# Two transformer blocks with a 32-expert layer: experts scattered in pairs, down weights laid out by partition, the first units split row by row, feed-forward features multiplied by the norms as they leave their banks

## The reference, cut to what matters

```python
# first block, x: 256 tokens by 1024
h = rms_norm(x, norm_mix);  z = h @ w_in                  # gated unit and differential attention
x = x + concat(a_out, o) @ w_out
x = x + memory_attention(rms_norm(x, norm_xq), rms_norm(mem, norm_mem), ...)
h = rms_norm(x, norm_ffn)                                 # 32 experts, 4 groups of 8
# the best group, its best two experts; wts = gate_g * pe_top / sum(pe_top)
y_e = (silu(h @ w_gate[e]) * (h @ w_up[e])) @ w_down[e]   # 1024 -> 512 -> 1024, chosen tokens only
x = rms_norm(x + sum_k wts[k] * y_ek, norm_final)
# second block
u = block_attention(rms_norm(x, norm_mix_pre_2));  h = x + rms_norm(u, norm_mix_post_2)
u = square(relu(rms_norm(h, norm_ffn_pre_2) @ w_up_2)) @ w_down_2    # 1024 -> 4096 -> 1024
out = h + rms_norm(u, norm_ffn_post_2)
```

## Time and profile before

| | |
|---|---|
| median of 3 runs | 1034.48 us (1034.04 to 1034.89) |
| the profiled execution | 1031.15 us, span 1029.7 us |
| PE, PEld, DVE, ACT, POOL busy | 94%, 63%, 40%, 33%, 2% |
| HBM read | 287.90 MB, 281 GB/s over the span |

### The profile page before, as it was taken

One profiled execution on the slowest core, in us unless ns is written; L12 is line 12 of the kernel. 1 busy time (PEld: TensorE's weight loads), 2 busy tenths in 40 slices (PEclk: granted clock), 3 DMA queues, 4 the chain that ended last, 5 costly groups with the idle time before them and its releaser, 6 DMA issues.

```text
span 1029.7 us, 13765 instructions
## 1 busy us (share of the span) xinstructions
PE 967.3 (94%) x5479; PEld 646.3 (63%) x5479; DVE 416.4 (40%) x721; ACT 339.4 (33%) x556; POOL 24.1 (2%) x40
## 2 busy tenths in 40 slices
PE   5999989998899999999999999997999969999997
PEld 4979878985433343333433334332898859998885
DVE  4756565445221212212222122223564655665434
ACT  7635436533111111111111111114464545454332
POOL 1300000000000000000000000000000000000000
PEclk9989999998999999999999999998999989999999
DMA  9943443486799999999999999999545525555501
GB/s 323 353 137 123 164 134 143 157 301 274 307 416 425 423 419 421 425 424 418 421 425 419 420 424 425 420 420 362 188 164 164 164 85 175 171 202 169 201 1 41
DMA packets 84047, 289.59 MB, mean 281 GB/s; under 512 B 4897, under 2 KB 44449, under 8 KB 75810
## 3 DMA queue, kind: packets, MB, share of 16 engines
q1 hardware_dynamic: 83426, 288.79, 73.3%
q10 hardware_dynamic: 576, 0.17, 0.1%
HBM read 287.90 MB, written 1.05 MB: 281 GB/s over the span
## 4 chain that ended last, share of the span: by engine, by line
PE 87%; DVE 6%; ACT 3%; issue 2%; POOL 1%; DMA 0%; DVEq 0%; SPq 0%; ACTq 0%
PE bank L1482 22%; PE bank L425 14%; PE bank L426 14%; PE bank L427 13%; PE bank L1503 11%; PE bank L1456 5%; PE bank L1514 2%; PE bank L1493 1%; DVE routeT L1578 1%; DVE w_low L506 1%; PE bank L708 1%; PE bank L746 1%; PE bank L467 1%; DVE arena L1577 1%; ACT w_high L477 1%
## 5 line engine op out<-in xcount | busy, mean ns | idle before, releaser
L506 DVE TENSOR_TENSOR w_low<-ring,w_high 128x2048 fp32r<-128x2048 f32 x78 | 178.9, 2294 | 135.2 <-ACT w_high L477 135.2
L1482 PE MATMUL bank<-ring,arena 128*64 128x512 f32 x1024 | 227.0, 595 | 0.0
L477 ACT ACTIVATE w_high<-ring 128x2048 fp32r<-128x2048 f32 x78 | 149.4, 1916 | 127.3 <-PE bank L427 127.3
L1482 PEld LDWEIGHTS bank<-ring,arena 128*64 128x64 f32 x1024 | 74.0, 138 | 145.1 <-issue 144.9
L1503 PE MATMUL bank<-ring,arena 128*64 128x512 f32 x512 | 116.9, 599 | 0.5 <-issue 0.5
L425 PE MATMUL bank<-xT_high,w_high 128*128 128x256 f32 x384 | 110.1, 287 | 2.4 <-DVE xT_low L515 2.4
L427 PE MATMUL bank<-xT_high,w_low 128*128 128x256 f32 x384 | 109.3, 285 | 0.0
L426 PE MATMUL bank<-xT_low,w_high 128*128 128x256 f32 x384 | 109.2, 284 | 0.0
L1588 DVE SCALAR_TENSOR_TENSOR y_low<-bank,arena,y_high 128x512 fp32r<-128x512 f32 x32 | 24.0, 751 | 135.8 <-ACT y_high L1545 135.8
L1584 DVE TENSOR_TENSOR arena<-bank,arena 128x256 f32<-128x256 f32 x32 | 13.6, 424 | 160.5 <-ACT arena L1534 160.5
L1534 ACT ACTIVATE arena<-bank 128x256 f32<-128x256 f32 x32 | 12.3, 384 | 196.4 <-PE bank L1482 196.4
(11 more groups left out here) (270 smaller groups left out, 1453.9 us busy)
## 6 DMA issues: line engine op xcount, KB each, us to landing
ring<-in_w_gate SPq DMA_DIRECT2D x32, 2048.0 KB, 18.6
ring<-in_w_up SPq DMA_DIRECT2D x32, 2048.0 KB, 23.1
ring<-in_w_down SPq DMA_DIRECT2D x32, 2048.0 KB, 21.7
ring<-in_w_up SPq DMA_DIRECT2D x16, 1024.0 KB, 5.7
ring<-in_w_down SPq DMA_DIRECT2D x16, 1024.0 KB, 4.9
ring<-in_attn_w_qkv SPq DMA_DIRECT2D x12, 1024.0 KB, 11.9
ring<-in_w_in SPq DMA_DIRECT2D x10, 1024.0 KB, 11.1
ring<-in_w_kv_mem SPq DMA_DIRECT2D x8, 1024.0 KB, 5.3
```

The costliest lines, as they stand in the source:

```text
L477: SC.activation(parts[buffer[0][u]][0][:, :], lanes[n % len(lanes)], ACT.Copy).then_inc(*high.inc(u))
L506: DVE.tensor_tensor(p[1][:, :], lanes[n % len(lanes)], p[0][:, :].bitcast(F32), ALU.subtract).then_inc(*split.inc(u))
L1482: last = PE.matmul(GU[t * SLOTS:(t + 1) * SLOTS, 0:NGU], xs[:, k, :], wgu[:, :, k, t * (DE // JT):(t + 1) * (DE // JT)], start=k == 0, sto ...
```

## The change

**Start.** The first two units are split in four rows of 512 columns each, with semaphores of their own, and PE starts with the first row; the second group of chunks of the tokens is written after that. `u0` is multiplied before the memory tokens are transposed.

**Experts.** The scatter works on pairs of experts. The route of a pair is built as three blocks of 64 slots (first, second, first expert), so that one transpose gives both experts above each other in 128 partitions. `down` of the second expert of a pair writes its halves exchanged, and `y` is kept by column half, with the two experts in 64 partitions each. A pair is scattered in the step after it, with matmuls of 128 partitions. The route transposes stand before `gate_up`, and the gather's pieces in four steps of six (three steps have a gather and no scatter). `y_high` and `y_low` become two instructions of 64 partitions each.

**Down weights.** They are laid out by partition on the host, as gate and up are: one run of 16 KB for each partition.

**Second feed-forward.** The sums are transposed without their norms. The norms are spread over partitions (`norm_wide`), transposed on PE after `f1` (bank `r2`) and kept as a row `row2`. DVE writes relu times norm out of the bank in one instruction (`norm_kept`), and ACT squares this twice, once into a float32 tile and once as the high part. The sum of squares of a bank's first half is taken when that bank is closed, and the mean is formed before the second gain.

```diff
+fT00@4 fT01@5 fT10@6 fT11@7 f0 f1 r2 f2 f3 f4 f5 f6 f7 f8 f9 f10 f11 f12 f13 f14@0 f15@7
...
-    w_down = a["w_down"][0].rearrange("e (c p) n -> e p c n", p=P)
+    w_down = a["w_down"]
...
-    for name in ("w_gate", "w_up"):
+    for name in ("w_gate", "w_up", "w_down"):
         laid[name] = np.stack([by_partition(w) for w in np.asarray(inputs[name])[0]])
...
+                    if row_ready and h == halves[0]:
+                        PE.wait_ge(*row_ready[c])
...
+        def rows_high(u):
+            n = order1.index(u)
+            SC.wait_ge(lane1_sem[n], 16)
+            for c in range(4):
+                o = slice(512 * c, 512 * (c + 1))
+                done = row_high.inc(f"{u}{c}") if c < 3 else high1.inc(u)
+                SC.activation(parts1[buffer1[0][u]][0][:, o], lanes1[n][:, o], ACT.Copy).then_inc(*done)
...
-        turned_highs(bank1, "hT", 0, hT[0], G_MIX)
-        high("v.0")
-        turned_highs(bank1, "hT", 1, hT[0], G_MIX)
-        high("v.1")
+        turned_highs(bank1, "hT", 0, hT[0], G_MIX, groups=(0,))
+        rows_high("v.0")
+        turned_highs(bank1, "hT", 1, hT[0], G_MIX, groups=(0,))
+        turned_highs(bank1, "hT", 0, hT[0], G_MIX, groups=(1,))
+        turned_highs(bank1, "hT", 1, hT[0], G_MIX, groups=(1,))
+        rows_high("v.1")
+        high("u0")
...
-            o = (t * NY) % 512
-            for y in YS:
...
-                                 tile_position=(t * SLOTS, 0), skip_group_check=True)
+            for y in Y[t]:
+                last = PE.matmul(ACC[2 * h + t][:, :], ROUTET[:, b, t, h, :], y[:, :], start=False, stop=True,
+                                 skip_group_check=True)
...
+        turn_route(q, n, b, odd, pair + 1, n)
...
-        if more and s:
-            gather_even(q, trio + 1, 2 * s - 2, 1 - buffer)
-        if more:
-            turn_route(q, n + 1, (j + 1) % 3, n)
-        scatter(q, n - 1, (j + 2) % 3, 0, False)
-        turn_hidden(q, n, n + 2 if more else n + 1)
-        scatter(q, n - 1, (j + 2) % 3, 1, True)
-        if more and s:
-            gather_odd(q, trio + 1, 2 * s - 1, 1 - buffer)
...
+        if p is not None:
+            gather_even(q, trio + 1, p, 1 - buffer)
+        if not odd:
+            scatter(q, n, n, (b + 2) % 3, 0, False)
+        turn_hidden(q, n, n + 1)
+        if not odd:
+            scatter(q, n, n, (b + 2) % 3, 1, True)
+        if p is not None:
+            gather_odd(q, trio + 1, p + 1, 1 - buffer)
...
+        for i in range(JT):
+            p, t = slice(i * SLOTS, (i + 1) * SLOTS), i ^ odd
+            last = SC.activation(Y[t][0][p, :], DN[p, 0:NY], ACT.Copy, scale=SLOT_WEIGHT[p, b, t:t + 1])
...
+        for i in range(JT):
+            p, t = slice(i * SLOTS, (i + 1) * SLOTS), i ^ odd
+            last = DVE.scalar_tensor_tensor(out=Y[t][1][p, :], in0=DN[p, 0:NY], scalar=SLOT_WEIGHT[p, b, t:t + 1],
+                                            in1=Y[t][0][p, :].bitcast(F32), op0=ALU.mult, op1=ALU.subtract)
+        last.then_inc(*q.inc("y"))
...
-            square_sum(X[:, h, :], XN[:, h, :], f"pre{h}", stat("pre", h))
-            scale_half("pre", h, XN, X)
...
-            SC.activation(scratch(2 * (i % 2)), banks[bank2.bank[f"f{i}"]][:, :], ACT.Relu).then_inc(*relu_done.inc(i))
...
-            SC.activation(hidden_parts[0][:, 512 * i:512 * (i + 1)], scratch(2 * (i % 2) + 1), ACT.Copy).then_inc(*sq_high.inc(i))
+            SC.activation(square, kept, ACT.Square)
+            SC.activation(hidden_parts[0][:, 512 * i:512 * (i + 1)], kept, ACT.Square).then_inc(*sq_high.inc(i))
...
-            DVE.tensor_tensor(scratch(2 * (i % 2) + 1), banks[bank2.bank[f"f{i}"]][:, :], scratch(2 * (i % 2)),
-                              ALU.mult).then_inc(*bank2.inc(f"f{i}"))
...
+            DVE.scalar_tensor_tensor(
+                out=scratch(2 * (i % 2)).rearrange("p (n t) -> p n t", t=S),
+                in0=banks[bank2.bank[f"f{i}"]][:, :].rearrange("p (n t) -> p n t", t=S), scalar=0.0,
+                in1=row2.rearrange("p (n t) -> p n t", n=1).to_broadcast([P, 2, S]), op0=ALU.max,
+                op1=ALU.mult).then_inc(*bank2.inc(f"f{i}"))
...
+                if j == 1:
+                    DVE.tensor_scalar(s[:, 0:1], s[:, 0:1], s[:, 1:2], RMS_EPS, ALU.add,
+                                      ALU.add).then_inc(*meansq.inc(f"{tag}{h}"))
```

380 lines of the change are left out of this document (223 added, 157 removed).

## The result

The changed kernel takes 1016.94 us (median of 4 runs, 1015.87 to 1017.38), the kernel before 1034.26 in the same comparison (1033.57 to 1034.89). The ratio is 0.9844, 95% interval 0.9827 to 0.9861: faster by 1.6%. Forecast were 1025.0 and a range of 1019.5 to 1031.0. The sign was right, the size too small, and the range did not hold the time.

A forecast was written before the change was run, and what follows sets the result against it. PE bounds the kernel, but the experts' loads leave only 2.0 us of slack. From 1031.15, −2.7 − 7.8 + 2.0 + 0.7 − 1.7 = −9.5 gives 1021.6, and the step to the median 1025.0; range 1019.5 to 1031.0.

The forecast's parts named there:

- the landing of the last `w_up`: End of the experts' stage: lands at 687.7 and starts the last `gate_up`, 10.5 us earlier, 7.8 the experts' own.
- the price of the feed-forward's loop: Second feed-forward: period 6.1 for 5.76, 0.37 more in 13 turns, 0.7 in the last two; whole part +0.7 us.
- Bound and mechanism: Experts: of PE's saving only 2.0 us of slack count unless transfers get faster; the last `w_up` sets the end.
- The third rival: Pairing and layout both buy nothing, freed time goes to new waits: −1.7 us, 1032.8; chance 0.08.
- the first (the layout buys nothing): Rival in the experts' loads: down piece no faster, last `w_up` 5.0 later, total −4.5 us, 1030.0; chance 0.13.
- The second, nothing of the start given back and a shorter loop: Rival at start and feed-forward: start keeps all, loop keeps 5.9 (−1.3 − 3), about 1020.5 us; chance 0.13.
- The down piece: Experts' loads: a down piece takes 4.92 us in place of 5.10, 5.0 us over 28 experts.
- the experts' two rates: Experts: PE saves 0.5 us for each, then waits for DMA about 0.85 us each in the last eight or so.
- The start: First matmul of `v.0` 3.4 us earlier, at 11.9; 0.7 given back behind it, so −2.7 us net.
- The tail: Behind the last `down`: doubled `y_high` and `y_low` cost 0.60 and 0.75, last scatter 0.6; 2.0 us later.
- From the profile to the median: Last step of the sum: 3.3 us added because before's median lay above its profiled execution, 1021.6 to 1025.0.
- The slower rival: Feed-forward loop: PE stands about 0.6 us each turn, clock drops, 15 turns cost 20 us, 1045; chance 0.06.

The follow-up runs named there:

- the four corners of layout and pairs: Kernels with neither, the new layout alone, pairs alone (changed, old layout), or both; first to last `gate_up` took 446.58, 446.14, 442.99 and 436.39 us.
- the run with half of the scatter: Changed kernel with the scatter of the low parts of `y` left out; 1020.12 us, ratio to the kernel before 0.9873.
- before's second profile: The kernel before, run again with a profile and no edit; 1032.3 us (one run).
- the changed kernel's second profile: The changed kernel, run again with no edit; 1015.58 us, ratio to the kernel before 0.9828.

## Why the prediction was right in sign and wrong in size

Four steps of the sum failed, against 8.1 us of miss: the landing of the last `w_up` (687.7, it was 685.8), PE's own saving in the experts (0.5 us for one, it was 0.33), the price of the feed-forward's loop (7.75 us given back, it was 4.5), and the 3.3 us added from the profile to the median (it was −0.4). The experts' own part, to which the first two belong, came out 2.4 better than forecast, the loop 3.2 and the step to the median 3.8; the other terms took 1.3 back.

**Bound and mechanism: right, by 0.3 us.** The last `gate_up` starts at the landing of the last `w_up`, as forecast, though PE stands only 0.33 us for it. That PE's saving alone counts little more than the slack, and that the layout is what turns it into time, is shown by the four corners of layout and pairs and by the run with half of the scatter. The third rival (both buy nothing) and the first (the layout buys nothing) are out. The second, nothing of the start given back and a shorter loop, came in its second half.

**The down piece: right, a little small.** Forecast 4.92 in place of 5.10, measured 4.89 in place of 5.11 (medians of the landings from 290 us on). The step from there to the stage failed: "The last `w_up` then lands at 696.2 − 2.7 − 0.8 − 5.0 = 687.7". It landed at 685.83. The 696.2 was one execution's, and held 1.5 us of a disturbance at 348 and 1.0 more at 287; the same kernel's second profile lands at 694.63. The down pieces gave 6.2 in place of 5.0. Against these, the queue began to fill only 1.5 us earlier (261.13 in place of 262.62), where 3.5 were forecast. 687.7 − 2.5 − 1.2 + 2.0 is 686.0, close to what was measured. A landing late in a filled queue carries every gap ahead of it, and gaps should be taken out before it is used as a base.

**PE alone: the experts' two rates, wrong.** 0.5 us for an expert was forecast, 0.33 measured (83.75 for six). The route's transposes cost 0.47 in place of 0.4, the steps that only gather 3.1 in place of 3.0, the ones that only scatter 2.3 in place of 2.2; the one that does both took 4.0, 4.2 were forecast. Over 30 experts that is 5.1 us: PE alone reaches the last `gate_up` at 685.6, not at 680.5. So PE did not stand 0.85 us in the last eight experts but 0.33 in the last one, and by the prediction's own sign ("if there is none ... the step of the experts' two rates is wrong") that step failed. That the time still came out from the loads is luck: PE was 5.1 later than forecast, the loads 1.9 earlier, and they met. The sign for the whole, an experts' stage that ends 5 to 9 us earlier, was just missed: the first transposes behind it come 9.39 earlier, the last `gate_up` 12.26.

**The start: right.** 3.20 of 3.4, and 1.13 given back where 0.7 was forecast; it is all lost by 53 us, ahead of the attention. The run with the old start and before's second profile put the net gain at the 2.30 us wait at 2.9, before's first profile at 2.1; 2.7 was forecast.

**The tail: 2.9 in place of 2.0.** Its steps are right: the first scatter matmul stands 15.65 us behind the last `gate_up` in place of 14.25, so the two doubled instructions cost 1.40 where 1.35 was forecast. The rest is clock: the granted clock is 0.66 from 702.36 to 704.03, and the last scatter matmuls come 0.43 us apart in place of 0.23. In the run with the old layout it is 1.00 there, and the transposes stand 23.18 us behind the last `gate_up`, in before's second profile 21.07: 2.1 later, as forecast. An instruction on 64 partitions takes as long as on 128: 0.683 us in the mean on ACT and 0.750 on DVE in the changed kernel, 0.687 and 0.751 before.

**The feed-forward: the loop is the mis-sized term.** "`f0` ... −7.05" came out as −5.55: the time from the last sums' end to `f0` is 2.54 (2.5 forecast), but the stretch up to them lost 1.6 us to PE's lower clock behind the 1.83 us wait at 780.21 (granted clock 0.64 up to 785.00, and 1.00 in the kernel before over the same instructions). Where the clock did not fall, in eight other profiles with this part, `f0` stands 43.85 to 43.88 behind `v1` in place of 51.00: 7.1 earlier, and the forecast's 7.05 is right. The +1.35 in the table is luck of the same kind: before's clock was 0.50 from 719.02 to 725.00, the changed kernel's was back at 1.00 from 713.30 on, and in the changed kernel's second profile the same distance is 71.99 us, where before has 71.93. In the loop "two squares of 0.60 each" is the step that cost most: the row's duration is not the distance to the next start on a filled engine. That distance is 0.54 and 0.52, and DVE's product takes 0.71 to the square. Summed, 6.1 became 5.91. PE alone needs 5.76 for a unit, not the 5.4 that the text took from the other shape of matmul: 48 of 256 columns come 0.12 apart, and PE stood in no turn of before's loop. So the loop's price was 0.16 and not 0.37 a turn. With the waits of 0.77 at `f3` and 0.55 at `y0` the loss is 4.1 up to `y0` and 0.45 in the `y` units, where 7.75 was forecast: the changed kernel is 3.2 us faster there than the forecast had it.

**From the profile to the median: wrong.** 3.3 us were added because before's runs lay that much above its profiled execution. The changed kernel's runs lie around its own (1017.38 to a median of 1016.94). The offset lay between executions of one kernel, as its two heaps 3.1 us apart show, and was not the program's. Had it been left out, the forecast would have been 1021.6, and 4.7 of the miss of 8.1 us would be left.

**The slower rival.** It supposed stands of 0.6 us in each turn. PE loses 0.16 us, and no turn's clock falls:

```profile
863.00:900.00 37.00, 37.00 (x302) 36.25 (x301) 22.46 (x20) 18.27 (x19) 0.00 (x0) 1.00 0.56 172
```

This window of the changed kernel has a clock of 1.00 over six units. What stands of 0.6 us would have done is not shown.

## What to carry to other kernels

Where an engine and a queue run nearly level, a change to one can show little and a change to both far more than the sum (0.4 and 3.6 us here, and 10.2 together); read the slack at the end of the stage, and clean the landing times of their gaps, before pricing either. On a filled engine sum distances from start to start around the whole loop, for the shape that runs there, and not the durations of its rows. If a loop feeds itself through two engines, take what depends on the unit just finished ahead of what prepares a later one.

## What the runs showed of the hardware that was not expected

- In a filled queue a 2 MB load landed 4.89 us behind the one ahead of it in runs of 16 KB, 5.11 in runs of 4 KB and 5.41 in runs of 2 KB; the DMA share read 1.01 to 1.02 in all, so that share doesn't tell of it, the GB/s do (428, 421, 413).
- After a wait of PE of about 2 us its clock was at the 1.2 GHz level for some microseconds in some executions and not in others, for the same instructions. Behind the 2.30 us wait in the first block it fell in 4 of 13 profiles (2.8 us more in two, 1.7 in two), behind the 1.83 us wait at `v1` in 2 of 13 (1.6 more). That it needs a wait of some length isn't shown; the 0.16 us lost in each turn of the loop never brought it. Differences under 3 us between two profiles of such a kernel need the clock's windows beside them.
